# A hybrid decoder step on one core: the first projection unit run by pairs of k tiles, as the adaLN shift and scale blocks land

## The chip, the core and the metric

The kernel runs on one NeuronCore of a Trainium2 chip. Its five engines run their own instruction streams and meet at semaphores: TensorE (PE, with its weight loads as PEld), VectorE (DVE), ScalarE (ACT), GpSimd (POOL) and SyncE (SP, which here only issues DMAs). The metric is the device time of one launch, in microseconds. Before the change the median of three runs is 2652.04 us (2644.44 to 2654.88).

## The reference, cut to what matters

One inference step of a two-layer decoder trunk, for a prompt of 1024 tokens and for 32 sample tokens (8 sequences of 4), all in float32. The change touches only the head of it:

```
mod = (silu(c) @ ada_w[layer] + ada_b[layer]).reshape(N, 6, 1, 1024)
h   = _rmsnorm(x, norm_mix_g[layer]) * (1 + mod[:, 1]) + mod[:, 0]
proj = h @ e_w_in        # layer 0: columns in blocks of 256: a_lin, a_gate, then q, k, v of three groups
glu  = proj[..., :256] * sigmoid(proj[..., 256:512])
```

`_rmsnorm` divides a token's row by the root of the mean of its squares, and multiplies by a gain per channel. `c` has one row for the prompt and eight for the samples (9 in all). Then come a causal convolution, windowed attention with a relative bias, an output projection, a SwiGLU FFN, and a second layer with other mixers.

## The kernel before, in words

**Layout.** Activations lie feature-major: 8 k tiles of 128 channels, each 1056 tokens wide (1024 of the prompt, 32 of the samples), processed in 3 blocks of 352. Each float32 product is made of three fp32r matmuls (high part times high, high times the weights' low part, low part of the activations times high). A projection unit is 256 output columns: 2 output tiles x 8 k tiles x 3 products x 3 blocks = 144 matmuls. Its weights (1 MB) are loaded by SP into one of three `w_raw` slots; ACT makes the high part (`split_hi`, L951) and POOL the low part in place (`split_lo`, L1928).

**Order of work.** `make_plan()` writes one list of items; every engine walks the same list and does its own part of each item, so an engine's order is the plan's order. `ahead()` is SP's order (the same list, but for the token stores). PSUM has 8 banks: six form two `big` tiles used in turn, two are `misc` banks used in turn. Whoever writes one waits until the reader of its last use has let go (`big_free`, `misc_free`).

**The head.** SP loads the identity, `pair_sum`, twelve small vectors and the rows of c, then the first adaLN block, then the tokens (8 tiles of 128 tokens x 1024 channels, 512 KB each, and the samples). POOL issues six loads of tables for the relative bias. An adaLN unit (`ada`, k = 0 to 7 here: shift blocks 0 to 3, scale blocks 4 to 7) is 1 MB of `ada_w`: PE multiplies it with silu(c), ACT copies the result (`ada_rows`, L1099), and in `ada_out` PE sums the parts (L2281) and DVE adds the bias into `mod` (L1539). Beside the eight `ada` items the tokens are transposed, one `x_in` item per k tile (L2246), copied to `x` by ACT or DVE (L1105, L1515), squared by ACT (L963) and summed by DVE (L1315). `rel_tables` builds the bias tables: PE L2253 and L2260, DVE L1522 to L1532; POOL then stores the samples' table (`d_bias`, L1971).

**The first norm.** The `norm` item finds the mean of the squares by matmuls (L2179, L2195), the root on ACT (L1001), spreads it by a matmul with a diagonal (L2202), and then makes, block by block, `nt` (DVE L1372), `h_hi` (ACT L992 to L996) and `h_lo` (DVE L1398 for even k tiles, POOL L1949 for odd ones). `project_as_made` (L2116) runs the first unit (`a_gate`) block by block as they come. Before that POOL has stored `x` to scratch (`d_x`, L1976) and then the relative bias rows (`d_rel`, L1979, 3 DMAs).

**After it.** Unit 1 (`a_lin`), unit 2 (v of group 0), unit 3 (k of group 0), unit 4 (q of group 0), each dense on PE (L2087). In unit 3, when the first of its two tiles is ready, DVE's `leave` (L1441) waits for both scratch stores, since `qk_fm` lies over `x`. The token transposes of v (L2360) run among the pieces of unit 3 and are copied by DVE (L1685). SP loads unit u+1 when it meets unit u, and waits for its slot.

Of the kernel before, what the change touches and what calls it, by code (L numbers as in the profile page):

```python
# [27 lines left out]
F32 = mybir.dt.float32  # L28
# [152 lines left out]
def make_plan():  # L181
# [66 lines left out]
    items.append(Item("setup", vec=take("misc"), c=take("misc"), ext=take("misc")))  # L248
    for k in range(KT):
        ada()  # L250
        if k == 0:
            tables = Item("rel_tables", rel=take("misc"), rels=take("misc", 2))
            items.append(tables)
        items.append(Item("x_in", k=k, x=take("big")))
    ada_out()
    items.append(Item("rel", of=tables))
# [7 lines left out]
    items.append(Item("norm", layer=0, which=0, n=take("norm"), misc=take("misc", 3)))  # L264
    dense("project", "e_w_in", 1, role="a_gate", first=0)
# [163 lines left out]
def build_trunk(nc: bass.Bass, A: dict, O: dict):  # L429
# [25 lines left out]
    def keep(name, shape, dt=F32):  # L455
# [41 lines left out]
    vrow = at("vrow", R_HH, [P, 3, P])  # L497
    tab = at("tab", R_HH + 1536, [N_BUCKETS + 1, 12])
    oh_p = at("oh_p", R_HH + 8192, [N_BUCKETS + 1, 3, REL])
    oh_s = at("oh_s", R_HH + 12800, [N_BUCKETS, 6, 160])  # L500
    mask_s = at("mask_s", R_HH + 16640, [P, 3, 160])
    row_step = at("row_step", R_HH + 18560, [P, NS])
    bias_s0 = at("bias_s0", R_HH + 18592, [P, 3, 160])
    tab_s = at("tab_s", R_HH + 20512, [N_BUCKETS, 3, HPG, S_TOK])
    ada_rows = [at("ada_rows0", R_HH + 25600, [P, 256]), at("ada_rows1", R_X + 32768, [P, 256]),
                at("ada_rows2", small[0] - 2048, [P, 256])]
    sq_first = at("sq_first", R_HL + 18432, [P, TOK])
# [67 lines left out]
    with ExitStack() as ctx:  # L575
# [26 lines left out]
        in_loaded, x_loaded, tabs_loaded = sem("in_loaded"), sem("x_loaded"), sem("tabs_loaded")  # L602

        raw_loaded = [sem(f"raw_loaded{s}") for s in range(NRAW)]
# [11 lines left out]
        sq0_made, sq0_summed = sem("sq0_made"), sem("sq0_summed")  # L616
# [60 lines left out]
        def hi_made(e, n, turn, k):  # L677

            e.wait_ge(nhi_act, 24 * n + 8 * turn + k + 1)

        def lo_made(e, n, turn, k):

            e.wait_ge(h_dve if k in LO_DVE else h_pool, 12 * n + 4 * turn + k // 2 + 1)
# [18 lines left out]
        def norm_turn(n, turn):  # L702

            return 3 * n + turn + 1

        def rows_at(k):

            return 0 if k < 8 else 1 if k < 24 else 2

        ada_outs = [it for it in plan if it.kind == "ada_out"]  # L710
        x_tiles = [it.x for it in plan if it.kind == "x_in"]

        use_at = {(it.of or it).unit: i for i, it in enumerate(plan) if (it.of or it).unit is not None}
        raw_of, raw_last, raw_turns = {}, [None] * NRAW, []

        def take_raw(freed, free_at):

            slot = min(range(NRAW), key=lambda s: raw_last[s].free_at if raw_last[s] else -1)
            old = raw_last[slot]
            raw_turns.append(slot)  # L720
            raw_last[slot] = Raw(len(raw_turns), slot, raw_turns.count(slot), old.freed if old else None, freed, free_at)
            return raw_last[slot]

        for i, it in enumerate(plan):
            if it.kind == "ada":
                it.raw = take_raw((misc_ready, it.misc + 1), i)
                continue
            u = 0 if it.kind == "rel" else (it.of or it).unit + 1 if it.kind in ("project", "down") or it.begins else None
            if u in unit_end:
                raw_of[u] = take_raw(unit_end[u], use_at[u])  # L730

        norms = {it.n: it for it in plan if it.kind in ("norm", "bound")}
# [66 lines left out]
        def _(sp):  # L799
# [15 lines left out]
            sp.dma_start(ident, A["ident"]).then_inc(in_loaded, 16)  # L815
            sp.dma_start(pair_sum, A["pair_sum"]).then_inc(in_loaded, 16)
            for part, names in enumerate((
                    ("ada_b",), ("norm_mix_g", "norm_ffn_g", "final_norm_g"),
                    ("a_conv_w", "a_conv_b", "a_ln_g", "a_ln_b", "c_conv_w", "c_conv_b", "d_ln_g", "d_ln_b"))):
                row = 0  # L820
                for name in names:
                    flat = A[name]
                    if len(flat.shape) == 2:
                        flat = flat.rearrange("a b -> (a b)")
                    elif len(flat.shape) == 3:
                        flat = flat.rearrange("a b c -> (a b c)")
                    k = flat.shape[0] // P
                    sp.dma_start(vrow[row:row + k, part, :], flat.rearrange("(r n) -> r n", n=P)).then_inc(in_loaded, 16)
                    row += k
            sp.dma_start(c_rows[0:1, :], A["c_prompt"]).then_inc(in_loaded, 16)  # L830
            sp.dma_start(c_rows[1:9, :], A["c_sample"]).then_inc(in_loaded, 16)
# [65 lines left out]
            for it in ahead():  # L897
                if it.kind == "rel":
# [3 lines left out]
                elif it.kind == "ada":  # L902
                    if it.k == 1:
                        for n in range(8):
                            sp.dma_start(x_tok[:, n, :], A["x_prompt"][0, n * P:(n + 1) * P, :]).then_inc(x_loaded, 16)
                        sp.dma_start(xs_tok, A["x_sample"].rearrange("b s d -> (b s) d")).then_inc(x_loaded, 16)
# [1664 lines left out]
```

## Time and profile before

| what | us |
|---|---|
| median of 3 runs | 2652.04 |
| the profiled execution, own time | 2646.14 |
| its span in the profile | 2644.4 |
| PE busy | 2531.3 (96%) |
| weight loads busy | 2401.8 (91%) |
| DVE / ACT / POOL busy | 939.5 / 590.2 / 510.7 |
| first product of unit 0 starts | 64.37 |
| unit 1 starts | 96.01 |

The profile is of one execution. Times in it count from the start of its span. "Busy" adds up the instructions of an engine; matmuls overlap, so a busy PE is not a full one. The granted clock of TensorE stands beside stretches (1.00 is 2.4 GHz, 0.50 is 1.2 GHz).

### The profile page before, as it was taken

The numbers are of one execution on the slowest core, as the hardware profiler recorded it, in microseconds if no ns is written. First come the engines' busy times: TensorE is split into PE (matmuls) and PEld (weight loads), VectorE is DVE, ScalarE is ACT, GpSimd is POOL, SyncE is SP. The second block draws the span as 40 slices with busy tenths as digits, with TensorE's granted clock in tenths as the row PEclk, the third lists the DMA queues.
The fourth block names the chain that finished last, engine by engine and source line by source line (L and its number), as shares of the span: only waits on it lengthen the run. The fifth ranks groups of instructions, "written<-read, shape, count | busy, mean of one in ns | idle before, by whom it ended". The sixth has DMA issues, their size and how long they took to land.

```text
span 2644.4 us, 36622 instructions
## 1 busy us (share of the span) xinstructions
PE 2531.3 (96%) x16305; PEld 2401.8 (91%) x16305; DVE 939.5 (36%) x1694; ACT 590.2 (22%) x908; POOL 510.7 (19%) x197
## 2 busy tenths in 40 slices
PE   6998889889999999999999999999999999999998
PEld 4997777668999999999999899989999999999997
DVE  4376653456122221212224512536222222222225
ACT  3312223425211111111112411044311111111112
POOL 2321001102222112212212322112322221122220
PEclk8999999899999999999999999999999999999999
DMA  9522332771212212222221578311111111011101
GB/s 316 74 70 87 97 108 88 237 256 34 77 51 80 96 65 80 80 78 67 80 92 52 181 252 294 114 43 33 32 48 48 49 48 48 32 49 48 49 32 66
DMA packets 165112, 246.75 MB, mean 93 GB/s; under 512 B 7451, under 2 KB 152257, under 8 KB 163803
## 3 DMA queue, kind: packets, MB, share of 16 engines
q1 hardware_dynamic: 151078, 179.41, 20.7%
q0 software_dynamic: 5456, 60.83, 7.6%
q10 hardware_dynamic: 8420, 4.15, 0.6%
q8 instruction: 129, 2.11, 0.3%
q14 instruction: 29, 0.23, 0.0%
HBM read 225.69 MB, written 62.52 MB: 109 GB/s over the span
## 4 chain that ended last, share of the span: by engine, by line
PE 73%; DVE 3%; ACT 2%; DMA 1%; issue 1%; SPq 0%; DVEq 0%
PE ps L2087 66%; PE ps L2159 3%; PE ps L2273 1%; PE ps L2116 1%; DVE h_lo L1398 1%; DMA cache<-in_cache_b_kv 1%; DVE x L1333 1%; DMA w_raw<-in_e_w_out 0%; PE ps L2186 0%; ACT h_hi L992 0%; ACT nt L994 0%; DVE nt L1372 0%; PE ps L2281 0%; PE ps L2316 0%; DVE ln_t L1728 0%
## 5 line engine op out<-in xcount | busy, mean ns | idle before, releaser
L1928 POOL TENSOR_TENSOR w_lo<-w_raw,w_hi 128x2048 fp32r<-128x2048 f32 x93 | 432.9, 4654 | 1790.9 <-ACT w_hi L951 1790.9
L2087 PE MATMUL ps<-h_hi,w_hi 128*128 128x352 f32 x2976 | 657.0, 329 | 7.4 <-DVE h_lo L1423 3.4
L2087 PE MATMUL ps<-h_hi,w_lo 128*128 128x352 f32 x2976 | 643.3, 324 | 0.0
L2087 PE MATMUL ps<-h_lo,w_hi 128*128 128x352 f32 x2976 | 642.8, 324 | 0.0
L2087 PEld LDWEIGHTS ps<-h_hi,w_hi 128*128 128x128 f32 x2976 | 503.4, 190 | 27.0 <-issue 22.6
L2087 PEld LDWEIGHTS ps<-h_hi,w_lo 128*128 128x128 f32 x2976 | 512.4, 188 | 0.0
L2087 PEld LDWEIGHTS ps<-h_lo,w_hi 128*128 128x128 f32 x2976 | 507.6, 189 | 0.0
L1418 DVE SCALAR_TENSOR_TENSOR x<-ps,mod,x 128x704 f32<-128x704 f32 (+1 forms) x384 | 270.5, 746 | 289.3 <-PE ps L2087 289.3
L1464 DVE TENSOR_TENSOR tmp<-ps,tmp 128x1056 f32<-128x1056 f32 x44 | 55.3, 1258 | 722.7 <-PE ps L2087 722.7
L951 ACT ACTIVATE w_hi<-w_raw 128x2048 fp32r<-128x2048 f32 x93 | 177.7, 1911 | 515.4 <-PE ps L2087 355.1
L2087 PE MATMUL ps<-mid_hi,w_hi 128*128 128x352 f32 x1104 | 242.2, 328 | 5.9 <-DVE acc_s L1419 5.2
L2087 PE MATMUL ps<-mid_hi,w_lo 128*128 128x352 f32 x1104 | 239.3, 324 | 0.0
L2087 PE MATMUL ps<-mid_lo,w_hi 128*128 128x352 f32 x1104 | 238.9, 325 | 0.0
L2087 PEld LDWEIGHTS ps<-mid_hi,w_hi 128*128 128x128 f32 x1104 | 188.8, 190 | 12.2 <-issue 6.3
L2087 PEld LDWEIGHTS ps<-mid_hi,w_lo 128*128 128x128 f32 x1104 | 190.8, 189 | 0.0
L2087 PEld LDWEIGHTS ps<-mid_lo,w_hi 128*128 128x128 f32 x1104 | 188.6, 189 | 0.0
L956 ACT ACTIVATE tmp<-ps 128x1056 f32<-128x1056 f32 x52 | 54.4, 1052 | 446.2 <-PE ps L2087 435.7
L1030 ACT ACTIVATE mid_hi<-tmp 128x1056 fp32r<-128x1056 f32 x44 | 47.9, 1088 | 426.5 <-DVE tmp L1464 426.5
L1539 DVE TENSOR_TENSOR mod<-ps,vecs 128x18 f32<-128x18 f32 x48 | 8.2, 172 | 242.9 <-PE ps L2281 242.9
L1653 DVE SCALAR_TENSOR_TENSOR conv_a<-ext_p,vecs,conv_a 128x1024 f32<-128x1024 f32 x60 | 85.0, 1416 | 0.0
L2116 PE MATMUL ps<-h_hi,w_hi 128*128 128x352 f32 x192 | 67.5, 354 | 11.2 <-ACT h_hi L992 5.3
L1949 POOL TENSOR_TENSOR h_lo<-nt,h_hi 128x352 fp32r<-128x352 f32 (+1 forms) x48 | 45.5, 952 | 111.7 <-ACT h_hi L996 111.7
(295 smaller groups left out, 2065.7 us busy)
## 6 DMA issues: line engine op xcount, KB each, us to landing
w_raw<-in_ada_w SPq DMA_DIRECT2D x48, 1024.0 KB, 6.8
w_raw<-in_ffn_w_gate_up SPq DMA_DIRECT2D x44, 1024.0 KB, 5.1
out_kv_sample<-in_cache_b_kv POOLq DMA_DIRECT2D x8, 4088.0 KB, 20.3
w_raw<-in_ffn_w_down SPq DMA_DIRECT2D x22, 1024.0 KB, 5.0
cache<-in_cache_b_kv SPq DMA_DIRECT2D x28, 512.0 KB, 6.0
w_raw<-in_e_w_in SPq DMA_DIRECT2D x11, 1024.0 KB, 5.5
w_raw<-in_o_w_in SPq DMA_DIRECT2D x10, 1024.0 KB, 13.4
out_kv_sample<-in_cache_b_kv POOLq DMA_DIRECT2D x8, 1016.0 KB, 8.0
```

The costliest lines, as they stand in the source:

```text
L951: act.activation(w_hi[u % 2], w_raw[r.slot], ACT.Copy).then_inc(w_hi_done, 1)
L956: return act.activation(blocks(dst), big(t)[:, :, 0:BLK], func, **kw).then_inc(big_free[t % 2], 1)
L1030: act.activation(mid_hi[:, it.j % 2, m, :], tmp[:, m, :], ACT.Copy).then_inc(hid_hi, 1)
L1333: ins = dve.scalar_tensor_tensor(x[:, m, c], big(t)[:, bank, 0:c.stop - c.start], mod[:, 6 * d.layer + d.gate, m, 0:1], x[:, m, c], ALU.mu ...
L1418: dve.scalar_tensor_tensor(dst, src, g, dst, ALU.mult, ALU.add)
L1464: dve.tensor_tensor(blocks(tmp[:, m, :]), T[:, :, 0:BLK], blocks(tmp[:, m, :]), ALU.mult)\
L1653: ins = dve.scalar_tensor_tensor(dst, src, w, dst, ALU.mult, ALU.add)
L1928: pool.tensor_tensor(w_lo[raw_of[u].slot], w_raw[raw_of[u].slot], w_hi[u % 2].bitcast(F32), ALU.subtract)\
L1949: pool.tensor_tensor(h_lo[:, k, c], nt[:, k, c], h_hi[:, k, c].bitcast(F32), ALU.subtract).then_inc(h_pool, 1)
L2087: mm = pe.matmul(big(t)[:, b, 0:BLK], wt, xt[:, k, b * BLK:b * BLK + BLK], start=(k == 0 and n == 0), stop=(k == K - 1 and n == 2))
L2116: return pe.matmul(big(t + m)[:, b, 0:BLK], halves[s][:, k, m * P:m * P + P], xt[:, k, b * BLK:b * BLK + BLK], start=(k == 0 and step == 0 ...
L2159: mm = pe.matmul(big(t + i)[:, bank, 0:BLK], halves[s][:, k, m * P:m * P + P], xt[:, k, c], start=(k == 0 and n == 0), stop=(k == 1 and n ...
```

## The change

The tokens are now loaded first by SP, before everything but the identity and the rows of c; the twelve vectors and `pair_sum` are issued by POOL, ahead of the tables. Each token tile is squared and summed along its row by ACT (one activation with an accumulated output), and transposed by PE for all 8 k tiles at once into two PSUM banks. The roots are taken in four groups of two or three token tiles, spread by a matmul with a diagonal, and `xr` = x times the inverse root is made by DVE, one token tile at a time. Then unit 0's weights are split, and the adaLN units come in pairs p and 4 + p (shift and scale of the same two k tiles). `first_h` makes the h of these two k tiles; `first` runs unit 0's products over them. The loads have five more `w_raw` slots for this (over `w_hi1` and over the token tiles already used). The old `x_in`, `rel` and `norm` items are gone, POOL makes no `h_lo` in this unit, and the scratch stores come after both splits and after the last adaLN unit, `d_rel` first and `d_x` behind it.

```diff
+    take("norm")
+    items.append(Item("setup", c=take("misc")))
+    for tile in range(9):
+        items.append(Item("x_tile", n=tile))
+        if tile == 7:
+            items.append(Item("vectors", vec=take("misc")))
+        if tile in (2, 4, 6, 8):
+            items.append(Item("x_roots", n=tile // 2 - 1, misc=take("misc")))
+    gate = Item("project", weights="e_w_in", col=1, unit=take("unit"), big=take("big", 2), role="a_gate")
+    items.append(Item("first_weights", of=gate))
+    # first_adas(p): ada for k in (p, 4 + p); first_rows(p): ada_out for both, then first_h(k=p)
...
+    first_adas(0)
+    first_rows(0)
+    items.append(Item("rel_tables", rel=take("misc"), rels=take("misc", 2), ext=take("misc")))
+    for p in range(4):
+        items.append(Item("first", of=gate, k=2 * p, which="high", begins=p == 2))
+        if p < 3:
+            first_adas(p + 1)
+        items.append(Item("first", of=gate, k=2 * p + 1, which="high"))
+        if p < 3:
+            first_rows(p + 1)
+        items.append(Item("first", of=gate, k=2 * p, which="low", ends=p == 3))
+    items.append(Item("first_stores"))
...
 # ACT
+                elif it.kind == "x_tile":
+                    x_square(it.n)
+                    # after tiles 1, 3, 5, 8: Sqrt of the group's sums
...
+                    if it.n == 8:
+                        for n in (4, 5, 8):
+                            x_copy(n)
+                    elif it.n in (2, 3, 4, 5):
+                        x_copy(it.n - 2)
+                elif it.kind == "first_weights":
                     split_hi(0)
+                elif it.kind == "first_h":
+                    for k in (2 * it.k, 2 * it.k + 1):
...
+                        act.activation(h_hi[:, k, 0:SEQ], xr[:, k, 0:SEQ], ACT.Identity, bias=mod[:, 0, k, 0:1],
+                                       scale=mod[:, 1, k, 0:1]).then_inc(first_hi, 1)
...
 # DVE
+                elif it.kind == "x_roots":
+                    rooted(it, 0)
+                    for i, n in enumerate(ROOTS[it.n]):
+                        c = x_tokens(n)
+                        if n in (6, 7):
+                            dve.wait_ge(x_turned, n + 1)
+                            own(dve.tensor_copy(x[:, :, c], x_turn(n)))
...
+                        dve.tensor_tensor(xr[:, :, c], x[:, :, c], ...).then_inc(xr_made, 1)
+                    root_used(it, 0, (xr_made, n + 1))
+                elif it.kind == "first_h":
...
+                    for k in (2 * p, 2 * p + 1):
+                        dve.wait_ge(first_hi, k + 1)
+                        own(dve.tensor_scalar(xr[:, k, 0:SEQ], xr[:, k, 0:SEQ], mod[:, 1, k, 0:1], mod[:, 0, k, 0:1],
+                                              ALU.mult, ALU.add))
+                        dve.tensor_tensor(h_lo[:, k, 0:SEQ], xr[:, k, 0:SEQ], h_hi[:, k, 0:SEQ].bitcast(F32), ALU.subtract)\
+                            .then_inc(first_lo, 1)
...
+                elif it.kind == "rel_tables":
                     dve.wait_ge(tabs_loaded, 16 * 6)
                     dve.tensor_copy(tab_s, ...).then_inc(tab_made, 1)
                     dve.wait_ge(misc_ready, it.rel + 1)
...
 # POOL
+                elif it.kind == "first_stores":
+                    for a in ada_units[6:8]:
+                        pool.wait_ge(misc_ready, a.misc + 1)
+                    pool.wait_ge(raw_loaded[raw_of[1].slot], 16 * raw_of[1].turn)
...
                         pool.dma_start(d_rel[HPG * g:HPG * g + HPG]...).then_inc(rel_stored, 16)
...
+                    pool.dma_start(d_x, x.rearrange("p k n -> p (k n)")).then_inc(x_stored, 16)
...
 # PE
+            def first_products(it):
...
+                if it.which == "high":
+                    if it.k == 0:
+                        pe.wait_ge(w_lo_done, u + 1)
...
+                    pe.wait_ge(first_hi, it.k + 1)
+                    pe.wait_ge(first_s_hi, it.k // 2 + 1)
+                    for m in range(2):
+                        for s in range(2):
+                            for b in range(3):
+                                pe.matmul(big(t + m)[:, b, 0:BLK], halves[s][:, it.k, m * P:m * P + P], ...)
+                    return
+                # "low": for m, for k in (k, k + 1): wait first_lo, then 3 blocks
...
+                elif it.kind == "x_tile":
...
+                    pe.wait_ge(x_loaded[n], 16)
+                    if n >= 3:
+                        pe.wait_ge(x_copied, n - 2)
+                    for k in range(KT):
+                        mm = pe.transpose(x_turn(n)[:, k, :], ...)
...
                 elif it.kind == "rel_tables":
                     pe.wait_ge(tab_made, 1)
...
 # SP
+                    if it.raw.slot >= 4:
+                        sp.wait_ge(x_turned, 2 * (it.raw.slot - 4) + 2)
+                        sp.wait_ge(x_squared, 2 * (it.raw.slot - 4) + 2)
```

Unit 1's weights are asked for at the `first` item with `begins` (k tile 4), between the third and the fourth pair, into the slot that adaLN unit 4 used; the same item splits them on ACT and POOL. Unit 2's go into the slot of adaLN unit 7, unit 3's into unit 0's.

## Rows read from the trace of the kernel before

**Rows 1.** The page: busy us of each engine, share of the span, instructions.

```profile
PE 2531.3 (96%) x16305; PEld 2401.8 (91%) x16305; DVE 939.5 (36%) x1694; ACT 590.2 (22%) x908; POOL 510.7 (19%) x197
```

**Rows 2.** Busy us per stretch by engine, then granted clock, DMA share, GB/s.

```profile
36.00:48.70 12.70, 12.06 (x122) 8.35 (x121) 8.71 (x14) 8.23 (x14) 0.00 (x0) 1.00 1.10 348
64.30:68.40 4.10, 4.03 (x12) 3.46 (x13) 3.75 (x7) 3.49 (x8) 2.50 (x3) 0.50 1.04 396
68.40:94.95 26.55, 24.76 (x145) 22.37 (x144) 18.57 (x28) 17.23 (x32) 13.68 (x11) 1.00 0.67 49
96.05:119.60 23.55, 23.55 (x146) 23.55 (x147) 1.96 (x6) 2.56 (x2) 4.60 (x1) 1.00 0.52 63
119.60:144.00 24.40, 24.40 (x155) 24.32 (x154) 12.62 (x18) 3.10 (x4) 5.65 (x1) 1.00 0.34 81
```

**Rows 3.** Timeline of the head: start us, us, engine, line, instruction, idle before.

```profile
6.42 0.27 SPq L831 DMA_DIRECT2D c_rows<-in_c_sample  x1
9.95 1.06 ACT L1090 ACTIVATE c_rows<-c_rows 9x1024 f32<-9x1024 f32 x1 [7.86 <-DMA c_rows<-in_c_sample]
14.86 1.45 PE L2253 MATMUL ps<-oh_p,tab 33*4 33x383 f32 x6
16.37 1.68 DVE L1522 COPY new_qk<-ps 4x383 f32<-4x383 f32 x3 [2.15 <-PE ps L2253]
20.52 0.49 DVE L1532 TENSOR_TENSOR bias_s<-ps,mask_s 128x320 f32<-128x320 f32 x1
23.44 1.97 PE L2246 MATMUL ps<-ident_sb,x_tok 128*128 128x128 f32 x8 [3.38 <-DMA xs_tok<-in_x_sample]
36.26 0.61 PE L2281 MATMUL ps<-pair_sum_sb,ada_rows 128*128 128x9 f32 x4
36.88 1.07 PE L2273 MATMUL ps<-w_raw,cs 128*32 128x256 f32 x16
52.30 4.50 POOL L1928 TENSOR_TENSOR w_lo<-w_raw,w_hi 128x2048 fp32r<-128x2048 f32 x1 [30.36 <-ACT w_hi L951]
53.13 3.75 DVE L1323 SCALAR_TENSOR_TENSOR mod<-mod,vecs 128x72 f32<-128x72 f32 x1
55.39 1.28 ACT L1001 ACT_TABLE_LOAD   x1
```

**Rows 4.** Groups by line and shape: busy us, mean ns of one, idle before.

```profile
L1315 DVE TENSOR_TENSOR tmp<-tmp 128x1024 f32<-128x1024 f32 x4 | 4.9, 1217 | 1.6 <-ACT tmp L963 1.6
L1675 DVE TENSOR_SCALAR tmp<-cext_p,vecs 128x1024 f32<-128x1024 f32 x4 | 3.2, 807 | 0.0
L963 ACT ACTIVATE tmp<-x 128x1024 f32<-128x1024 f32 x5 | 5.3, 1058 | 11.8 <-DVE x L1516 11.7
L992 ACT ACTIVATE h_hi<-nt,mod 128x352 fp32r<-128x352 f32 x32 | 18.5, 578 | 12.5 <-DVE nt L1372 12.5
```

**Rows 5.** DMA issues (KB each, median us to landing), unit 3's load last.

```profile
scratch_x<-x POOLq DMA_DIRECT2D x1, 4224.0 KB, 15.5
scratch_rel<-new_qk POOLq DMA_DIRECT2D x3, 766.0 KB, 50.1
w_raw<-in_e_w_in SPq DMA_DIRECT2D x1, 1024.0 KB, 38.2
```

**Rows 6.** The tile `scratch_rel`: issues, and landing times.

```profile
L1979 POOL DMA_DIRECT2D scratch_rel<-new_qk x3: 1082/1106/1142, 57.3 to 59.6; - x3
DMA to landing us min/median/max: 3.4/10.0/75.3
```

**Rows 7.** Timeline of unit 3 and its weights, as rows 3.

```profile
133.15 1.92 ACT L951 ACTIVATE w_hi<-w_raw 128x2048 fp32r<-128x2048 f32 x1 [34.54 <-DMA w_raw<-in_e_w_in]
135.15 5.65 POOL L1928 TENSOR_TENSOR w_lo<-w_raw,w_hi 128x2048 fp32r<-128x2048 f32 x1 [31.86 <-ACT w_hi L951]
155.82 1.35 DVE L1441 COPY qk_fm<-ps 128x352 f32<-128x352 f32 x3
160.42 0.38 PE L2360 MATMUL ps<-ident_sb,v_fm 128*128 128x128 f32 x2
```

More of the change, by code:

```diff
@@ L246, in among, with first_adas, first_rows @@
         return out
[L248 to L256, printed above, removed]
+    take("norm")
[8 more added lines that the diff above has]
+    items.append(Item("first_weights", of=gate))
+    def first_adas(p):
+        for k in (p, 4 + p):
+            ada_units.append(Item("ada", k=k, misc=take("misc")))
+            items.append(ada_units[-1])
+    def first_rows(p):
+        for k in (p, 4 + p):
+            items.append(Item("ada_out", k=k, misc=take("misc")))
+        items.append(Item("first_h", k=p))
+    first_adas(0)
[10 more added lines that the diff above has]
+    items.append(Item("first_stores"))
     def into_norm(weights, col, to, **kw):
@@ L1971, in _ @@
                     pool.dma_start(d_bias, bias_s0.rearrange("p g n -> p (g n)")).then_inc(bias_stored, 16)
-                elif it.kind == "rel":
+                elif it.kind == "first_weights":
                     split_lo(0)
-                    for t in x_tiles:
-                        big_evacuated(pool, t)
-                    pool.dma_start(d_x, x.rearrange("p k n -> p (k n)")).then_inc(x_stored, 16)
-                    misc_evacuated(pool, it.of.rel)
+                elif it.kind == "first":
+                    if it.begins:
+                        split_lo(1)
+                elif it.kind == "first_stores":
+                    for a in ada_units[6:8]:
+                        pool.wait_ge(misc_ready, a.misc + 1)
+                    pool.wait_ge(raw_loaded[raw_of[1].slot], 16 * raw_of[1].turn)
+                    tables = next(i for i in plan if i.kind == "rel_tables")
+                    misc_evacuated(pool, tables.rel)
                     for g in range(3):
@@ L2192, in mean_of @@
                 pe.wait_ge(part_copied, norm_turn(it.n, turn))
[L2193 removed]
                 for j in range(4):
[L2195 to L2196 removed]
+                    mm = pe.matmul(misc(it.misc + turn)[0:88, 384 + j:385 + j], parts_sb[:, turn % 2, 88 * j:88 * j + 88],
+                                   pair_sum[:, 0:1], start=True, stop=True)
                 mm.then_inc(mean_made, 1)
@@ L2263, in _ @@
                         mm.then_inc(misc_ready, 1)
+                    misc_slot(it.ext)
+                    for m in range(2):
+                        for half in range(2):
+                            at_ = 240 * m + 120 * half
+                            mm = pe.transpose(misc(it.ext)[:, at_:at_ + 120], st_rows[0:120, half, m * P:m * P + P],
+                                              ident[0:120, 0:120])
+                    mm.then_inc(misc_ready, 1)
                 elif it.kind == "ada":
```

377 lines of the change are left out of this document (201 added, 176 removed).

## The prediction, made before the changed kernel ran

> **What bounds the kernel now.** I read the page first: PE is busy 96% of the span, its weight loads 91%, and no other engine over 36% [rows 1]. So the kernel is a PE queue of dense units, and what the head is worth is the time at which the dense part starts. Next I cut the head into stretches [rows 2]. A dense unit takes 23.55 us (96.05 to 119.60, 144 matmuls, 0.1635 us each); unit 2 with its small guests takes 24.4. Between 68.40 and 94.95 unit 0 runs with gaps, and from 64.30 to 68.40 its 12 matmuls start at a granted clock of 0.50 (the 1.2 GHz level), after a stretch in which PE mostly waited for the norm. Unit 0 thus ends at 94.95, and unit 1 starts 1.10 later. The whole of unit 0 would fit in 23.5. Ahead of it, from 36.00 to 48.70, the loads run at 348 GB/s: one 1 MB adaLN block per 3.0 us, and everything follows them. After the last block come the norm and the first h: 48.7 to 64.4. The change attacks these two, the 16 us of norm after the last load and the wait for all eight blocks. Only the end of unit 0 counts, so I work out that instant, T0, in the new order. Then I look for what the new order makes late behind it.
>
> **Tokens and rows, to 35 us.** The loads start with tokens. The c rows are issued at 6.42 and used at 9.95 before [rows 3]. They now go out at about 2.6, behind two 512 KB tiles (3 us at the 348 GB/s of [rows 2]); 2.6 + 3.5 as before, and a little for the tiles, gives 6.5. All tokens are in by about 15 us, so they do not bound. ACT does: silu 1.06, to 7.6; nine squares by the 1.06 row for 1024 columns [rows 4], plus 0.1 each as my allowance for the accumulated output; the table load for Sqrt, 1.28 [rows 3]; seven copies out of PSUM of the same size, taken as a square. In plan order that gives copy 4 at 24.2 and copy 5 at 25.2. PE's tiles 7 and 8 wait for those two copies and end at 26.3 and 28.5. So copy 8 ends at 29.0 and unit 0's `split_hi` at 30.9, and POOL's split (4.50, [rows 3]) at 35.5. DVE must make xr, nine products of about 1.22 [rows 4] (PSUM is one input, none waits for POOL), and it copies tiles 6 and 7 itself (taken as the same 1.22). After copy 5: xr 4 and 5 to 26.7; vectors 27.7; diagonals of 6 to 8 at 28.6; their roots at 29.4; then 2 x (1.22 + 1.22) and 0.5: 34.9.
>
> **The first pair, to 41 us.** adaLN unit 4 needs the misc bank that root group 3 holds until DVE is through with xr 8, at 34.9. At the slow clock PE takes 1.94 for it (1.07 at full clock, [rows 3]): 36.9. Its block landed long before. ACT copies, PE sums the parts of both (0.61 at full clock, 1.0 slow) to 38.0, DVE adds and scales to 38.5. ACT makes h_hi of k tile 0: the slope of the 352 column row (0.578 us, [rows 4]) gives 1.2 for 1024, so 39.7, and k tile 1 at 41.1.
>
> **A wait the plan adds: the bias tables, 41 to 51 us.** `rel_tables` stands between the first pair and the first products. Its PE part waits for `tab_made`, and the copy that raises it is now in DVE's `rel_tables`, behind DVE's `first_h`, which makes both low parts of the pair. DVE: tensor_scalar 0.81, subtraction 1.22 [rows 4], twice, with the sample parts: 39.7 to 44.1; then the copy: 44.5. Behind PE's wait stand all products of unit 0. The tables themselves went from 14.86 to 21.01 before, in a ping-pong of PE and DVE over two misc banks [rows 3]: 1.45 + 1.68 + 2.95. The transposes of the convolution state now follow them in the same banks. I take 6.5 for PE: first product at 51. This block cost nothing before (it lay in the wait for the tokens); here it costs about 10 us of PE, which had its first h at 40.
>
> **Unit 0 in pairs, 51 to 88 us.** From here PE sums: 144 x 0.1635 = 23.5; six adaLN units at 1.07 = 6.4; six sums of parts at about 0.6 = 3.6. That is 33.5. All blocks are there: unit 1's load waits for adaLN unit 4 (36.9) and lands near 42.5, then the last two blocks at 45.5 and 48.5; PE wants them at 73. The first 12 matmuls at the slow clock cost more: 4.03 us for 12 before, against 1.96, is 2.1 [rows 2]; part of that row is waiting, and I take 1.5. Between pairs, PE has 1.96 of low products while DVE adds, scales, and ACT makes h_hi and the sample copy (0.2 + 0.2 + 1.2 + 0.3 + hand-overs 0.3 = 2.2): a gap of 0.3, three times. In pair 3 one more wait: unit 1's POOL split runs from about 74.5 for 4.5, and a DVE instruction with all inputs in SBUF does not run beside it. The row: a scale of 72 elements took 3.75 from 53.13, ending with POOL's 52.30 + 4.50 [rows 3]. DVE's scale of the fourth pair is due at 79.2 and POOL ends at 79 to 80.2: 1.3 us late. At the end the low parts of k tiles 6 and 7 come about as PE wants them. T0 = 51 + 33.5 + 1.5 + 0.9 + 1.3 = 88.2. Against 94.95: 6.8 us sooner. The bounds: 8 sooner still if PE never waits for the tables (first product at 43, the POOL split done at 35.5), 4 if the clock stays high and the port is free; 6 later if every PE step to 60 us is at the slow level and the ACT chain runs 3 us long.
>
> The Trainium skill, page "SBUF — State Buffer", section "Who interferes with whom", says that VectorE and GpSimd share one port pair which the first to issue holds for a whole instruction; with two SBUF inputs, or in a two-port mode, VectorE takes part in this. By it the order decides: if DVE's subtraction for k tile 5 starts just before POOL's split, POOL is late by 1.2 and the end moves by as much; with POOL first the sum is as above. The row of 3.75 us agrees.
>
> **What the later stores do, +2.6 us.** Before, POOL stored x at 56.8 (landed in 15.5) and then `d_rel` at 57.3 to 59.6. The last landed 75.3 after its issue, at 134.9 [rows 5, 6]. So `d_rel` by itself took 134.9 - 72.3 = 62.6 us. Now it goes out when POOL is through with unit 1's split, at about 80, and x goes behind it in the same queue. `d_rel` ends near 80 + 1 + 62 = 143, x near 153 (the last engine's share of 4.3 MB, 10 us by its 15.5 less some 3 of latency). Two things wait behind. First unit 3's weights: before, asked for at 94.97, landed after 38.2 [rows 5], split by 140.8 [rows 7], wanted at 144.0. The distance from T0 is the same in the new order (49 us; 38.2 + 7.7 = 45.9), so no stall if the load again takes its turns among the slow packets. Second, DVE's `leave` of unit 3, at 155.82 before [rows 7], T0 + 60.9; it is now due at 149 and waits for x until 153 to 154. Behind it are the copies of v's transposes. PE runs two of them without DVE, and the third, at 160.42 before [rows 7], now 153.6, waits until x + 2.0 = 155.6 to 156. So 2.6 us are given back. Bounds: nothing (x_stored by 149) to 12 (x at 166, if d_rel takes its whole 75.3 again and x its 15.5).
>
> "DMA: Bandwidth & Descriptors", section "Queues, rings and completion order", of the Trainium skill says that each DMA engine goes round between the queues that have work, a packet at a time. By it unit 3's load shares with `d_rel` and lands at 88 + 38 = 126. Served strictly behind it, it would land at 143 and PE would stall 14 us. The trace agrees with the turns: 38.2 us, and done before `d_rel`.
>
> **The sum.** -6.8 + 2.6 = -4.2, all against the profiled execution (2646.14, span 2644.4). From there to the end PE is dense and nothing of the change is in it: 2641.9. The profiled execution lies 5.9 below the median of the runs shown, whose fastest is 2644.44; -4.2 on the median is 2647.8. I give the time in between, towards the median: 2646.
>
> **Rivals.** (A) The forecast: a small gain, from 13 less to 6 more. Chance 0.6.
>
> (B) The overlap works as drawn: PE starts unit 0 as soon as h is there. For it: all data are in SBUF, PE has 10 us of pure waiting in my sum. Against it: the order of DVE's items. First product 42, T0 = 42 + 33.5 + 2.7 = 78.2, 16.7 sooner; stores and leave move together, so 2.6 come back: 2632 to 2634. If the row stage is also 8 us faster than my ACT chain, 2625. Chance 0.18.
>
> (C) The slower end: the two scratch stores, now 23 us later than before while their reader comes 7 sooner. One mechanism: DVE stands in unit 3's `leave` until x has landed, PE has no misc bank, and unit 4's first tile no PSUM. It decides from x landing after 151.6; each us beyond is a us. If `d_rel` needs 75 and x 15.5, x lands at 171: 19 of stall, less 6.8: +12.6, so 2662. For it: 50.1 median and 75.3 at most [rows 6], 50 GB/s in the stretch to 94.95 [rows 2]. Against it: in those 75.3 the first 15 were x's. Chance 0.12.
>
> (D) The change doesn't do what it says: the pairs run one after the other, as each h waits on a chain PE to DVE to ACT, and DVE's low parts (2 x 2.03 + samples, nearly 6 us per pair) hold the next pair's `mod`. 3 us of gap in each of the three hand-overs instead of 0.3, and T0 = 96.3: +1.4 and +1 to 2 by the stores: 2650. Against it: PE has 9 us of work per pair. Chance 0.1.
>
> **Numbers.** 0.5% is 13 us, about what a measurement of this kernel can tell from no change. Faster by more: all but a little of B (0.16) and the low end of A (0.04): 0.20. Slower by more: half of C and the tails of A and D: 0.11. The rest, 0.69, within. A's own range is 2633 to 2655; the range that takes in B's near end and most of C is 2628 to 2661.
>
> **What would show it.** In the new profile: the first matmul of `first_products` near 51 and idle PE before it released by DVE's table copy; adaLN unit 4 at 35, behind xr 8; unit 1's start near 89; POOL's split of unit 1 with a long DVE scale beside it; `d_rel` issued near 80; a DVE wait on `scratch_x` in `leave` near 149 to 154, and a PE gap of 2 to 3 us before a transposition of v_fm. It is wrong if the first product starts before 45 (B), if the DVE wait on the store passes 10 us (C), or if PE shows gaps over 2 us in each pair (D).

## The result, and the profile after

The kernel after takes 2659.68 us (median of 20 runs, 2653.43 to 2663.21), the kernel before 2647.09 in the runs beside them (20 runs, 2638.76 to 2656.39). The ratio is 1.0043, with a 95% interval of [1.0032, 1.0054]. My sum had said 4.2 less; it is 12.6 more. The profiled execution took 2660.36, its span 2658.6, against 2644.4 for the span before: 14.2 more.

The head did what it should, and a little more. This is the timeline of PE in the kernel after (start us, us, engine, line, instruction, idle before it and what ended it), with two rows of other engines among them; it answers [rows 3] and [rows 7].

```profile
36.16 1.94 PE L2398 MATMUL ps<-w_raw,cs 128*32 128x256 f32 x16 [3.58 <-DVEq L1407]
46.27 1.45 PE L2370 MATMUL ps<-oh_p,tab 33*4 33x383 f32 x6 [6.37 <-issue]
52.12 1.23 PE L2207 MATMUL ps<-h_hi,w_hi 128*128 128x352 f32 x3
81.57 0.72 PE L2207 MATMUL ps<-h_hi,w_hi 128*128 128x352 f32 x3 [0.98 <-ACT h_hi L1160]
88.06 0.72 PE L2173 MATMUL ps<-h_hi,w_hi 128*128 128x352 f32 x3 [0.27 <-ACT sig L994]
...
125.31 1.04 PE L2173 MATMUL ps<-h_lo,w_hi 128*128 128x352 f32 x3 [11.81 <-issue]
...
149.22 1.91 ACT L989 ACTIVATE w_hi<-w_raw 128x2048 fp32r<-128x2048 f32 x1 [58.53 <-DMA w_raw<-in_e_w_in]
151.21 5.49 POOL L1998 TENSOR_TENSOR w_lo<-w_raw,w_hi 128x2048 fp32r<-128x2048 f32 x1 [55.81 <-ACT w_hi L989]
...
156.75 1.25 PE L2173 MATMUL ps<-h_hi,w_hi 128*128 128x352 f32 x3 [7.09 <-POOL w_lo L1998]
```

Unit 1 starts at 88.06; before it was 96.01. That is 8.0 us sooner. Then two holes open. At 113.5 PE stops in the middle of unit 2 for 11.81 us, and no semaphore that the profile shows releases it. At 149.66 it stops again, 7.09 us, for unit 3's weights. The stretches show what each hole costs beyond its length (columns as in [rows 2]):

```profile
88.06:113.40 25.34, 25.34 (x156) 25.31 (x157) 3.60 (x9) 2.63 (x2) 4.62 (x1) 1.00 0.84 129
113.40:125.31 11.91, 0.10 (x1) 0.00 (x0) 0.10 (x1) 0.00 (x0) 0.00 (x0) 0.63 0.71 133
125.31:130.40 5.09, 5.09 (x20) 4.87 (x20) 0.00 (x0) 0.00 (x0) 0.00 (x0) 0.53 0.57 104
130.40:156.75 26.35, 19.26 (x121) 18.97 (x119) 13.07 (x18) 2.65 (x3) 5.49 (x1) 0.95 0.52 139
156.75:161.10 4.35, 4.35 (x15) 4.35 (x16) 0.00 (x0) 0.00 (x0) 0.00 (x0) 0.53 0.22 81
```

After each hole the granted clock is 0.53, which is nearly all of the stretch at 0.50, the 1.2 GHz level. Fifteen matmuls of 352 columns take 4.35 us there; at 0.1635 each they would take 2.45. So each hole costs some 1.9 us more. The account is -8.0 + 11.8 + 7.1 + 2 x 1.9 = +14.7. The first matmul of the attention is the mark behind which the two kernels do the same. It stands at 209.13 after and 193.79 before (+15.3), and the spans differ by 14.2.

Now the DMA side of the kernel after: first the issues (KB each, median us from issue to landing), of unit 3's load alone and of x.

```profile
w_raw<-in_e_w_in SPq DMA_DIRECT2D x1, 1024.0 KB, 61.4
scratch_x<-x POOLq DMA_DIRECT2D x1, 4224.0 KB, 78.5
```

Then the tile `scratch_rel`, as [rows 6]:

```profile
L2068 POOL DMA_DIRECT2D scratch_rel<-new_qk x3: 1108/1137/1163, 79.9 to 82.1; - x3
DMA to landing us min/median/max: 3.9/24.1/68.7
```

`d_rel` goes out at 79.9, as worked out, and its last part lands at 82.1 + 68.7 = 150.8. Unit 3's weights, asked for at 87.8, land 61.4 later, at 149.2. Before it was 38.2 [rows 5]. Put the two ends side by side. Before: weights 133.15, `d_rel` 59.6 + 75.3 = 134.9 [rows 6, 7]. After: 149.2 and 150.8. Both times the load lands some 1.7 us ahead of the end of `d_rel`. What I had read as a duration was an end.

### The profile page after: what moved, and what is told of

Same layout as the page of the kernel before. It is cut to its first block, busy times and chain, and to the rows that moved or that the text cites. A ratio compares the mean times of both kernels' runs of the same rounds, so it can differ in the third digit from the quotient of the medians.

```text
span 2658.6 us, 36563 instructions
## 1 busy us (share of the span) xinstructions
PE 2526.7 (95%) x16287; PEld 2404.0 (90%) x16287; DVE 929.8 (35%) x1682; ACT 584.6 (22%) x890; POOL 506.1 (19%) x198
## 4 chain that ended last, share of the span: by engine, by line
PE 73%; DVE 3%; ACT 2%; DMA 1%; issue 1%; SPq 0%; DVEq 0%
PE ps L2173 65%; PE ps L2273 3%; PE ps L2398 1%; PE ps L2230 1%; DVE h_lo L1441 1%; DVE x L1376 1%; DMA w_raw<-in_e_w_out 0%; PE ps L2296 0%; ACT h_hi L1037 0%; PE ps L2591 0%; ACT nt L1039 0%; DVE nt L1415 0%; PE ps L2406 0%; PE ps L2434 0%; DVE ln_t L1798 0%
## 5 line engine op out<-in xcount | busy, mean ns | idle before, releaser
L2173 PE MATMUL ps<-h_hi,w_hi 128*128 128x352 f32 x2976 | 659.0, 330 | 13.7 <-POOL w_lo L1998 7.1
L2173 PE MATMUL ps<-h_lo,w_hi 128*128 128x352 f32 x2976 | 644.8, 325 | 11.8 <-issue 11.8
L2398 PE MATMUL ps<-w_raw,cs 128*32 128x256 f32 x768 | 54.2, 405 | 9.7 <-DMA w_raw<-in_ada_w 4.4
L1466 DVE TENSOR_TENSOR mid_lo<-tmp,mid_hi 128x1056 fp32r<-128x1056 f32 x50 | 62.4, 1254 | 1.0 <-DMA out_kv_prompt<-v_tok 1.0
## 6 DMA issues: line engine op xcount, KB each, us to landing
out_kv_sample<-in_cache_b_kv POOLq DMA_DIRECT2D x8, 4088.0 KB, 20.2
```

The source lines that it names most:

```text
L1466: return dve.tensor_tensor(dst, src, hi.bitcast(F32), ALU.subtract)
L2173: mm = pe.matmul(big(t)[:, b, 0:BLK], wt, xt[:, k, b * BLK:b * BLK + BLK], start=(k == 0 and n == 0), stop=(k == K - 1 and n == 2))
L2398: mm = pe.matmul(misc(it.misc)[j:j + S_TOK, 0:256], cs[:, k, :], w[:, k, :], start=(k < 4), stop=(k >= 4), skip_group_check=True)
```

## The experiments

**Order or time of the stores (e1 to e3).** The first question was whether x behind `d_rel` in POOL's queue was at fault (theory ORDER), or the point in time at which `d_rel` starts (theory TIME). e1 swaps the two stores:

```diff
-  pool.dma_start(d_rel...) x3; pool.dma_start(d_x...)      # at first_stores, near 80 us
+  pool.dma_start(d_x...); pool.dma_start(d_rel...) x3
```

> The changed kernel with its two scratch stores in the old order: d_x, then d_rel, both still issued near 80 us. The changed kernel stalls twice: PE stands 11.8 us inside unit 2 (113.5 to 125.3) with nothing that it waits for by a semaphore, and 7.1 us before unit 3, whose weights landed 61.4 us after they were asked for (38.2 before). Theory ORDER: it is d_x behind d_rel that does it; an engine that is through with d_rel's packets goes on to d_x's large ones, so that the weights and PE's own instruction fetch take turns with both. Then with d_x first it is over by 98, the weights land within 38 to 45 us of the asking (by 133), both stalls are gone or under 2 us, and the run is some 8 us below the kernel before: ratio 0.997. Theory TIME: it is d_rel in flight while unit 3's weights and the fetch pass, in whatever order. Then both stalls stay, d_rel ends near 157 instead of 149, DVE waits for it in unit 3, and the run is at 1.004 or above.

2665.1 us, ratio 1.006 [1.004, 1.0081]. The hole without a releaser is gone, and PE waits 26.5 us for unit 3's weights instead. `d_rel` ends at 82.5 + 76.5 = 159.0 and the weights land at 155.0. So TIME has the weights and the total right, but not the first hole, which it had staying.

e2 puts `d_rel` ahead of unit 0's products and leaves d_x late:

```diff
   pool.dma_start(d_bias, ...)                 # rel_tables
+  pool.dma_start(d_rel...) x3                 # 54.9 us
```

> The changed kernel with d_rel issued as soon as its table is there (near 53 us, behind d_bias), d_x as in the changed kernel near 80. Theory TIME: d_rel is over by about 115, so unit 3's weights (asked for at 88) land by 120, no wait before unit 3, and the 11.8 us gap in unit 2 is gone or under 3: ratio 0.997. Theory ORDER: d_x still stands behind d_rel until 115 and then runs with the rest; the weights land 45 to 60 after the asking (133 to 148), and the gap in unit 2 stays at over 5: ratio 1.000 to 1.003.

2662.83 us, 1.0052 [1.0033, 1.0071]. The hole comes 37 us sooner, 22 behind the start of `d_rel`: PE stands 19.9 us in the middle of an adaLN unit, from 76.6 to 96.4. That is what neither theory had said: TIME had the hole gone, ORDER had 1.000 to 1.003. The hole held up all that follows, so the next load, unit 2's, was asked for only at 99.7. `d_rel` ended at 57.1 + 68.5 = 125.6, x went out at 100.3 and landed at 136.3, and the load landed at 135.4.

e3 leaves `d_rel` at 80.8 and puts d_x behind unit 0's split:

```diff
   elif it.kind == "first_weights":
       split_lo(0)
+      pool.dma_start(d_x...)                  # 36.0 us
```

> The changed kernel with d_x issued as soon as x is complete (near 36 us), d_rel as in the changed kernel near 80. Both theories: d_x takes some 12 us of the loads' bandwidth, the last adaLN block lands near 61 instead of 49, still ahead of PE's use at 73, so unit 1 starts near 88 as in the changed kernel. Theory ORDER: with no d_x behind d_rel the weights of unit 3 land 38 after the asking (126) and PE has no gap in unit 2: ratio 0.997. Theory TIME: both stalls stay, 1.002 to 1.005.

2658.97 us, 1.0032 [1.0018, 1.0046]. x lands in 15.9 us, and PE waits 20.2 us for unit 3's weights, which land at 150.1 (`d_rel` ends at 83.1 + 68.9 = 152.0). These are PE's longest waits in each of the three (waiter, tile, line, releaser: us in total, times, longest us), first e1:

```profile
PE ps L2173 <- POOL w_lo L1998: 26.5, 1, 26.5
```

e2:

```profile
PE ps L2398 <- issue: 19.9, 1, 19.9
PE ps L2173 <- POOL w_lo L1998: 7.4, 1, 7.4
```

e3:

```profile
PE ps L2173 <- POOL w_lo L1998: 20.2, 1, 20.2
```

The holes of after add up to 11.8 + 7.1 = 18.9, near the 20.2 of e3. The first hole had cost little of its own, because PE would have met the late weights anyway. e14 below shows it alone, at 8.4 us. ORDER falls: with x out of the way the loss stays. The time fits TIME (1.002 to 1.005), though of its two stalls only the one for the weights is left.

**Both stores early (e4).** This is the edits of e2 and e3 together.

> The changed kernel with both stores early: d_x near 36 us, d_rel near 53. Both theories say that the two stalls are gone: unit 1 starts near 88, unit 3 near 137, and the run is 8 us below the kernel before: 0.997 (2639 in a profiled execution of 2646). If the gap in unit 2 is no matter of the stores at all (third theory, a place in the program), it stays near 11.8 here, and the run is at 1.001.

2653.64 us (2649.26 to 2672.94), 1.0021 [1.0006, 1.0036]. Both theories had 0.997 here, and both missed. In the profiled execution (span 2671.2, so near the upper end of its runs) the block caught is the last adaLN block:

```profile
105.58 1.94 PE L2398 MATMUL ps<-w_raw,cs 128*32 128x256 f32 x16 [30.01 <-DMA w_raw<-in_ada_w]
```

This block was asked for at 49.1, 5 us ahead of `d_rel` (54.3), and landed at 105.5, while `d_rel` went on until 56.5 + 65.9 = 122.4. So a load asked for shortly ahead of `d_rel` can be caught too, and here it was complete 17 us before `d_rel` was.

**The old kernel with late stores (e6).** If time is the cause, it must do harm without any of the new head:

```diff
# kernel before, POOL
-  pool.dma_start(d_x...); pool.dma_start(d_rel...) x3      # item rel, 57 us
   lows(it, turn, (1, 3, 5, 7)); if turn == 1: split_lo(1)
+  pool.dma_start(d_rel...) x3; pool.dma_start(d_x...)      # 92 us
```

> The kernel before, with its old head; only POOL's two stores (d_rel, then d_x) are moved behind the norm's low parts, to about 91 us instead of 57. TIME (a 1 MB load asked for in the first 10 us of d_rel lands only near d_rel's end): unit 3's weights, asked for at 95, land 55 to 62 after that (150 to 157 instead of 133), PE stands 12 to 20 us ahead of unit 3, ratio to the kernel before 1.005 to 1.008. HEAD (what was lost belongs to the new head, its packed plan or its cold clock, and the stores are harmless): no stall ahead of unit 3, ratio 0.999 to 1.001.

2671.12 us, 1.0101 [1.0083, 1.0118]: worse than the change, since it has the late stores and not the early head. Both holes are there, and with no new head to blame:

```profile
PE ps L2087 <- issue: 13.4, 1, 13.4
PE ps L2087 <- POOL w_lo L1928: 7.6, 1, 7.6
```

The weights land at 161.0 and `d_rel` ends at 94.5 + 68.1 = 162.6. This is TIME, and more of it than the 1.005 to 1.008 expected. The edit also puts `d_rel` ahead of x, but e1 and e3 have already shown that the order is not the cause of the late weights.

**No `d_rel` at all (e10).** It has e3's early d_x; the three stores are left out, and the biases are read from the x scratch, so this kernel leaves out work and its results are not the right ones:

```diff
-  pool.dma_start(d_rel...) x3
-  src = d_rel[...].rearrange("h (p n) -> p h n", n=REL)
+  src = d_x[:, HPG * REL * g:HPG * REL * (g + 1)].rearrange("p (h n) -> p h n", n=REL)
```

> The kernel after with d_x issued at 36 and without the three d_rel stores; the biases are read from the x scratch instead, so many numbers of the right shape but not the right ones. TIME: unit 3's load lands within 5 to 10 us of being asked for, PE has no stall from 88 to the attention, ratio to before 0.996 to 0.998 (2637 to 2641). HEAD: the loss stays, ratio 1.002 to 1.005.

2637.61 us, 0.9972 [0.9959, 0.9985]. Unit 3's weights land 5.4 us after they are asked for (row below). PE does not stop between unit 1 and the attention, which starts at 187.68, 6.1 sooner than before. From e3 to e10 the ratio falls by 0.6%, some 16 us: that is the price of `d_rel` in this place.

```profile
w_raw<-in_e_w_in SPq DMA_DIRECT2D x1, 1024.0 KB, 5.4
```

**The tables moved (e7).** My sum had charged 10 us of PE to the tables ahead of the first products:

```diff
-  items.append(Item("rel_tables", ...))                # ahead of the first pair's products
   items.append(Item("first", of=gate, k=2 * p + 1, which="high"))
+  if p == 0: items.append(Item("rel_tables", ...))
```

> The kernel after, with the rel_tables item behind the second product of the first pair instead of ahead of the first. Both theories: the first product starts near 42 to 44 instead of 52, adaLN and sums fill PE. TIME: unit 1 starts near 80 (8 sooner than 88), and d_rel, its stalls and everything behind move with it, so the time falls by 6 to 9 against the kernel after: 2651 to 2654, ratio to before 1.001 to 1.002. Rival (the tables' DVE and ACT work hinders the pairs just as much in its new place): unit 1 at 86 to 88, ratio 1.003 to 1.005.

2656.68 us, 1.0041 [1.0028, 1.0055]: no gain to be told from the kernel after, as the rival had it. Its PE timeline says why:

```profile
42.26 1.22 PE L2208 MATMUL ps<-h_hi,w_hi 128*128 128x352 f32 x3 [2.07 <-ACT h_hi L1161]
...
52.55 1.96 PE L2378 MATMUL ps<-oh_s,tab_s 32*128 32x160 f32 x6 [0.78 <-DVE new_qk L1610]
54.45 1.06 PE L2386 MATMUL ps<-ident_sb,st_rows 120*128 120x120 f32 x4
...
57.37 3.87 PE L2217 MATMUL ps<-h_lo,w_hi 128*128 128x352 f32 x12
61.03 1.08 PE L2208 MATMUL ps<-h_hi,w_hi 128*128 128x352 f32 x3
...
87.34 0.71 PE L2174 MATMUL ps<-h_hi,w_hi 128*128 128x352 f32 x3 [0.27 <-ACT sig L995]
```

The first product starts 9.9 us sooner. But the tables' own matmuls (5.9 us in the kernel after, from 46.27 to 52.12) now stand behind it, and the twelve low products run at 3.87 us instead of 2.18. The second pair is 1.5 sooner, unit 1 only 0.7. `d_rel` goes out at 79.2 as before, and PE waits 18.7 for unit 3's weights.

**Unit 3's weights ahead of `d_rel` (e14, e9).** The slot that adaLN unit 5 leaves near 60 takes unit 3's block, so that SP asks for it right behind unit 2's, near 76. e14 is the kernel after with that alone:

```diff
+  w_lo += [None] + [at(f"w_lo{4 + i}", R_MH + 8192 * i, [P, 2048], F32R) for i in range(2)]
-  raw_of[u] = take_raw(unit_end[u], use_at[u], {0: 0, 1: 2}.get(u))
+  raw_of[u] = take_raw(unit_end[u], use_at[u], {0: 0, 1: 2, 3: 4}.get(u))
```

> The kernel after with one edit: unit 3's weights go into the slot that is free from about 60 and are asked for near 76, ahead of d_rel. The stores stay in their order near 80, d_rel then d_x. TIME: no stall ahead of unit 3, and the late x (162 in the kernel after) shows for the first time: DVE's leave of unit 3, due at 149, waits 8 to 13 us for it, and a gap without a releaser in unit 2 is no longer hidden behind late weights, but hides the wait for x in its turn. Total 8 to 13 given back, so about the time of before: ratio 0.999 to 1.002. Rival (the weights were the whole loss): as e9, ratio 0.997 to 0.9985.

2650.17 us, 1.0008 [0.9991, 1.0025]. The wait for weights is gone, and the hole without a releaser now stands in the open:

```profile
122.44 1.04 PE L2174 MATMUL ps<-h_lo,w_hi 128*128 128x352 f32 x3 [8.42 <-issue]
...
162.99 1.35 DVE L1485 COPY qk_fm<-ps 128x352 f32<-128x352 f32 x3 [2.24 <-issue]
```

The second row is DVE's `leave` of unit 3. x was issued at 83.8 and landed 79.1 later, at 162.9, so these 2.24 us are the wait for x that the prediction had priced at 2.6, though at 163 and not at 149. PE waits 1.2 us behind it. The total is as TIME said; the wait for x is not, which it had at 8 to 13.

e9 adds e3's early d_x.

> The kernel after with d_x issued at 36 (as in e3) and unit 3's weights loaded into a fifth slot that is free from about 60, so that they are asked for near 76 with unit 2's, ahead of d_rel at 80. TIME: they land by 90, no PE stall ahead of unit 3; unit 4's load, asked for near 88 instead of 112, lands near 148, split by 156, wanted at 161. Nothing is given back: time = before - 8 to -5, 2638 to 2642 beside 2647, ratio 0.997 to 0.998. Rival (the loss is a fixed toll of d_rel on whatever PE needs, instruction fetch included): a stall of 8 to 20 us appears ahead of unit 2, 3 or 4 or with no releaser, ratio 1.001 to 1.004.

2639.64 us, 0.9984 [0.9974, 0.9994]. This beats the kernel before. What is left shows in its DVE row: `leave` of unit 3 waits for the end of `d_rel`. PE stands 3.84 us behind it and then runs at a granted clock of 0.50 from 158.41 to 162.00. The attention starts at 194.38, 6.7 later than in e10. (The text on record for e12 adds 2.2 us to the 3.8. That is a wait for adaLN weights inside the attention, and it has nothing to do with `leave`: the kernel before has 2.15 us of it, e10 2.19 and e12 2.16.)

```profile
156.58 1.35 DVE L1485 COPY qk_fm<-ps 128x352 f32<-128x352 f32 x3 [7.90 <-DMA scratch_rel<-new_qk]
```

e11 is e9 with e7's edit.

> e9 and e7 together: unit 3's weights ahead, d_x early, and the tables behind the second product of the first pair. e7 alone brought unit 1's start from 88.1 to 87.3 only, so 0.5 to 1.5 us below e9: ratio to before 0.997 to 0.9985. Rival (the tables' new place lets d_rel meet other packets): a stall of over 5 us, ratio 1.000 to 1.003.

2639.66 us, 0.9973 [0.9956, 0.9991], not to be told from e9.

**Two units ahead, `d_rel` at 73 (e12).** This is e9 with the slots dealt anew, so that units 2 and 3 are both in before `d_rel` starts at 73.2 (they land at 68.5 and 72.5). x is stored at 35.6, as in e3:

```diff
-  FIRST_RAW = {0: 1, 4: 2, 1: 3, 5: 4, 2: 5, 6: 6, 3: 7, 7: 1}
+  FIRST_RAW = {0: 1, 4: 2, 1: 3, 5: 7, 2: 4, 6: 5, 3: 6, 7: 7}
-  {0: 0, 1: 2}.get(u)
+  {0: 0, 1: 2, 2: 1, 3: 4}.get(u)
...
   if it.begins:
+      for u in (2, 3): pool.wait_ge(raw_loaded[raw_of[u].slot], 16 * raw_of[u].turn)
+      pool.dma_start(d_rel...) x3
       split_lo(1)
```

> As e9, but units 2 and 3 are both loaded by about 70 (unit 2 into the slot that is free from 38, adaLN units 5, 2, 6, 3, 7 in other slots) and d_rel is issued as soon as both are in, near 70, ahead of POOL's split of unit 1. TIME: d_rel ends near 140 to 145, before DVE's leave of unit 3 is due at 148, so the 7.9 us wait of e9 and PE's 3.8 + 2.2 behind it go: 3 to 6 us below e9, ratio to before 0.996 to 0.998. FETCH (PE's instructions come by packets of 16 KB that wait behind d_rel's): the packet due near 90 comes 20 to 50 us late, and PE stands 5 to 20 us in unit 1 or 2 without a releaser: ratio 0.999 to 1.004.

2638.3 us, 0.9969 [0.9954, 0.9984]. From unit 1 to the attention no PE wait of over 1 us is left, and the attention starts at 187.37, as in the kernel without `d_rel`. The load asked for behind `d_rel` is now unit 4's. It takes 54.0 us and nobody waits:

```profile
143.41 1.92 ACT L990 ACTIVATE w_hi<-w_raw 128x2048 fp32r<-128x2048 f32 x1 [24.58 <-DMA w_raw<-in_e_w_in]
151.17 1.34 DVE L1485 COPY qk_fm<-ps 128x352 f32<-128x352 f32 x3
```

**`d_rel` from ACT's queue (e13).** This is e9, with the stores issued by `act` instead of `pool`.

```diff
-  pool.dma_start(d_rel...) x3                 # 80 us
+  act.dma_start(d_rel...) x3                  # 89 us
```

> As e9, but the three d_rel stores are issued by ACT (a hardware queue) near 87, behind its sigmoid copies of unit 0, instead of by POOL (a software queue) at 80. If the 63 to 72 us of d_rel are a matter of its 1536 rows read from 4 partitions at a time (the transfer itself), they stay, it ends near 155 and the time is that of e9 or 3 to 6 more: ratio 0.998 to 1.001. If they are a matter of POOL's queue, d_rel ends within 20 to 40 us, by 125, no wait is left and the time is that of e10: ratio 0.996 to 0.998.

2677.56 us, 1.0118 [1.0095, 1.0141], the worst of all. The three issues hold ACT for 46.9 us, unit 2's weights are split 46 us late, and PE waits 29.9:

```profile
89.09 46.90 ACTq L1172 DMA_DIRECT2D scratch_rel<-new_qk  x3
136.09 3.71 ACT L990 ACTIVATE w_hi<-w_raw 128x2048 fp32r<-128x2048 f32 x2 [45.95 <-issue]
```

DVE's `leave` still waits 10.2 us for `d_rel`, until 191.05, which is 102 us behind its first issue. So the other queue did not make it short. But a load got through beside it: unit 4's, asked for at 112.9, landed at 144.4. Neither of my two numbers had counted on the issuing engine.

## Why the prediction was wrong, step by step

- **Tokens, rows and first pair.** Right: adaLN unit 4 at 36.16 (34.9 worked out) behind DVE, first product at 52.12 (51), behind the tables. But the 10 us charged to the tables were not there to be had: e7 got back 0.7 at unit 1. This also takes away most of rival B, whose 10 us were those. (B's 2632 is counted from the profiled execution, C's 2662 from some 3 us above it.)
- **Unit 0 in pairs.** Right: unit 1 at 88.06 (89 worked out), a gap of 0.98 ahead of pair 3 (1.3). Rival D fell.
- **`d_rel` near 80, ending near 143.** Issued at 79.9 and ended at 150.8. I had subtracted the first 15 us, which were x's. From the last issue to the last landing it takes 75.3 (before) and 76.5 (e1) with x directly ahead of it, and 65.9 to 72.4 in the ten others that issue it from POOL. So x ahead of it costs some 7 us, not 15, and the 62.6 was short for all of them.
- **"No stall if the load again takes its turns among the slow packets."** This step failed. I carried the 38.2 us of before as if a load among these packets needed that long, and got 88 + 38 = 126. But here a load that is asked for behind `d_rel` lands when `d_rel` is nearly through. Landing of the first such load and end of `d_rel` were 133.2 and 134.9 before, 149.2 and 150.8 after, 155.0 and 159.0 in e1, 150.1 and 152.0 in e3, 161.0 and 162.6 in e6, 147.0 and 148.8 in e7, 150.5 and 152.5 in e14, 153.7 and 156.4 in e9, 149.8 and 152.5 in e11, 143.4 and 145.9 in e12. Not so in e2 (135.4 and 125.6, with x until 136.3), in e4 (105.5 and 122.4) and with the stores on ACT's queue in e13 (144.4 and 190.6). In the kernel before the load was asked for 38 us behind the first issue of `d_rel`, so its wait was short; in the kernel after, 8 us behind it. The change brought the store 23 us later and the load 7 sooner, and so made it nearly the full length. The wait is 61.4 - 38.2 = 23.2 us longer, and the slack in [rows 7] (split by 140.8, wanted at 144.0) covers 3.2 of it. Unit 3 starts at 156.75, which is 20.7 behind 144.0 - 8.0.
- **The size of that step.** -8.0 and +18.9 of standing and +3.8 of slow clock, where the prediction had +2.6. Served strictly behind `d_rel`, the weights were to land at 143 with 14 us of stall. That was the other branch of my own sum, and the nearer one. I dismissed it because the one duration at hand "agreed" with the first.
- **DVE's wait for x in `leave`.** The mechanism is real (2.24 in e14, 7.90 for `d_rel` in e9), but in the kernel after it is covered: unit 3 is itself late, and `leave` starts at 172.95, behind x, which landed at 161.8. Rival C gave 2662 and the time was 2659.7, but by another wait than its own: that nearness is luck, and so is it that the wide range, 2628 to 2661, drawn for C, holds the time. The prediction also contradicts itself here: with `d_rel` at 75.3 and x at 15.5 its bound has x at 166 and rival C has 171; 80 + 75.3 + 15.5 is 170.8.
- **A hole with no releaser** (11.8 us) was in none of my cases.

**Why the load ends with the store.** The section "Queues, rings and completion order" of the Trainium skill's "DMA: Bandwidth & Descriptors" says that each DMA engine goes round between its queues, a packet at a time. The prediction leaned on it, and the traces agree with the turns; what I got wrong is how long turns take beside slow packets. e4 shows it cleanest, since from 91 to 102.5 only a few packets of the caught load are left (queue: packets, MB, share of 16 engines):

```profile
q0 software_dynamic: 127, 0.36, 42.2%
q1 hardware_dynamic: 9, 0.01, 0.2%
```

The nine start at 91.03, 92.43, 93.90, 95.29, 96.69, 98.16, 99.55, 101.02 and 102.40. Each takes 0.046 us, and within 0.06 us of its start a packet of `d_rel` begins that takes 1.33 to 1.42. So the load gets one packet of 1,024 bytes for each packet of 4,596 bytes of `d_rel`, one in 1.4 us. In the kernel after, `d_rel` has 504 such packets; about a third take 0.34 us, a third 0.75 and a third 1.3 or more. The load has 1,024 packets. If these lie evenly on 16 engines (an estimate), that is 64 on each, and beside packets of 1.4 us they need 90 us, more than `d_rel` lasts. Such a load can only be complete when the long packets on the slowest engine are through. The last of them in the kernel after ends at 146.2, and the load is in at 149.2. In e4 only some 430 packets of the load were left at 58.4, when `d_rel` had hardly begun, and the load was done 17 us before it. In e13 the packets of `d_rel` had 1,532 bytes and took 0.21 to 0.24 us, and a whole load went by beside them between 112.8 and 144.4:

```profile
q10 hardware_dynamic: 497, 0.76, 22.2%
q1 hardware_dynamic: 1040, 1.05, 10.2%
```

The traces don't say which of the 16 engines a packet ran on, so the count per engine stays an estimate.

## What to carry to other kernels

A landing time read from one trace can be a duration or somebody else's end: look at what else was under way and when that ended, before you add it to a new start. Where two transfers take turns, ask how many packets each has left and how long one of the other's takes, not only how many bytes go. When an edit moves a slow store, list every load asked for within its life, in the new order, and load those ahead of it (e12: 7 to 8 us better than before, from a change that alone was 12.6 worse). A moved store is as much a part of the change as the work that it was moved for.

## What the runs showed of the hardware

**A slow store form.** In e2, from 62 to 94 us, `d_rel` had the DMA engines to itself. For comparison, e12's loads from 60 to 72 (queue: packets, MB, share of 16 engines). First e2:

```profile
q0 software_dynamic: 436, 1.56, 62.1%
```

e12:

```profile
q1 hardware_dynamic: 3115, 3.14, 81.2%
```

That is 32 x 16 x 0.621 / 1.56 = 204 us of engine time for a MB of `d_rel`, and 50 for a MB of weights. `d_rel` reads four partitions in each of its three DMAs, 128 times over; whether that is what makes it slow was not tried apart. From ACT's queue (e13) the same bytes went in 1,536 packets that took 348 us of engine time in all, where the 504 long ones of the kernel after took 494; yet the store was longer in the end.

**A PE hole and the instruction packets.** The profile lists packets of the kind "instruction". Without `d_rel` (e10) three of them move between 74 and 122 us: at 74, at 94 and at 112. In the kernel after there are none in that time, the next moves at 122, and PE's hole ends at 125.31. First e10, 74 to 122:

```profile
q1 hardware_dynamic: 3120, 3.15, 21.4%
q10 hardware_dynamic: 300, 0.28, 2.2%
q8 instruction: 3, 0.05, 0.4%
```

The kernel after, 74 to 122, all queues, and then 122 to 123:

```profile
q0 software_dynamic: 1607, 3.95, 62.3%
q1 hardware_dynamic: 1963, 1.98, 13.3%
...
q8 instruction: 1, 0.02, 5.5%
```

In e6 no such packet moves from 75.3 to 131; one does in the next us, and the hole ends at 134.12. In e2 there is none from 62 to 94, one in the next us, and the hole ends at 96.42. In e14 the packet moves at 120 and the hole ends at 122.44. In finer windows these packets start at 123.0, 131.7, 94.2 and 120.2, so each of the four holes without a releaser ends 2.2 to 2.4 us after the start of a late packet. The other end fits too: in the kernel after and in e14 the hole opens 40.6 us behind the packet before it (72.9 and 113.50; 73.4 and 114.02), while e3 (93.7 and 129.7), e11 (92.5 and 127.6) and e9 (74.5 and 110.9), where the next packet came within 37 us, have no hole. The kernel before has 42 us between two packets (73.4 and 115.6) and none either, but its PE waited at times in that stretch. That PE had run out of instructions is the reading that fits all of this; it is not shown, since the trace does not say whose instructions a packet holds. All four have x still to be stored when `d_rel` starts; e3, e4, e9 to e13, with x early, show no such hole, and e1, with x directly ahead of `d_rel`, shows none. But e7, with the order of the kernel after, shows none either: its packets moved at 93 and 109. So the order of the two stores does not decide it alone, and what does stays open.

**A DMA issue can hold its engine.** On POOL the three issues took 3.4 us. On ACT, in e13, they took 46.9, and ACT did nothing else from 90.1, when its two sigmoid copies ended, to 136.1.
